# Stick attention begins with the gate projection: a written-out opening of the stage's order

## The reference, cut to what matters

```
def _stick_breaking(q, k, v):                      # 8 heads of 64
    for blk in range(s // SB_BLOCK):               # 8 blocks of 128 queries
        z = einsum('bhqd,bhkd->bhqk', q[:, :, q0:end], k[:, :, :end]) * scale
        log_keep = where(mask, log_sigmoid(-z), 0.0)
        rest = cumsum(log_keep, axis=3, reverse=True) - log_keep
        a = where(mask, exp(log_sigmoid(z) + rest), 0.0)
        outs.append(einsum('bhqk,bhkd->bhqd', a, v[:, :, :end]))
...
q_b = swapaxes(_rms(qkv_b[:, :, 0], sb_q_gain), 1, 2)
k_b = swapaxes(_rms(qkv_b[:, :, 1], sb_k_gain), 1, 2)
o_b = o_b * silu(z_b)
o_a = _rms(o_a, dn_out_gain) * silu(z_a)
gates = sigmoid(proj[..., B_Z1:G1] + b_gate)       # 2048 columns of xn @ w_in
```

## Time and profile before

| | |
|---|---|
| median of 3 runs | 2778.96 us (2775.7 to 2780.8) |
| profiled execution, its own time | 2784.54 us |
| its span, first to last instruction | 2782.6 us |
| PE busy in the span | 2615.7 us (94%) |
| DVE, ACT, POOL busy | 1263.3, 938.4, 352.8 us |
| mean granted TensorE clock | 0.968 |
| stick phase: first instruction, last sigmoid of the gates | 685.56 us, 1056.33 us |

### The profile page before, as it was taken

The page is one execution under the profiler, slowest core; times in us unless marked ns, Lnnn a source line. Parts: engine busy times, 40 slices in busy tenths (PEclk is TensorE's granted clock), DMA queues, the critical chain, the costliest instruction groups (busy, mean ns, idle before and its releaser), DMA issues. The chain is left out here.

```text
span 2782.6 us, 36583 instructions
## 1 busy us (share of the span) xinstructions
PE 2615.7 (94%) x14702; PEld 2245.0 (81%) x14702; DVE 1263.3 (45%) x1770; ACT 938.4 (34%) x1549; POOL 352.8 (13%) x450
## 2 busy tenths in 40 slices
PE   8969999998799998999997989889999999999999
PEld 6849999997588886888886877767888888778877
DVE  6523444442466764543136858454233222323452
ACT  4223322221456652123115767532212111222331
POOL 1002232220332320001012223010000000000000
PEclk9979999999799998999998989989999999999999
DMA  4222121112333215443323211163222222355532
GB/s 144 86 75 82 53 77 49 53 43 64 103 117 92 74 56 185 148 137 101 122 97 102 56 41 39 35 215 92 68 69 76 71 81 68 112 180 171 189 102 80
DMA packets 215503, 264.71 MB, mean 95 GB/s; under 512 B 46852, under 2 KB 147844, under 8 KB 215336
## 3 DMA queue, kind: packets, MB, share of 16 engines
q1 hardware_dynamic: 215336, 262.38, 29.6%
HBM read 185.11 MB, written 77.22 MB: 94 GB/s over the span
## 5 line engine op out<-in xcount | busy, mean ns | idle before, releaser
L3801 PE MATMUL ffn_up_acc<-mixed_hi,ffn_ring_hi 128*128 128x512 f32 x704 | 274.9, 390 | 2.5 <-DVE mixed_lo L2922 2.5
L3801 PE MATMUL ffn_up_acc<-mixed_hi,ffn_ring_lo 128*128 128x512 f32 x704 | 274.6, 390 | 0.0
L3801 PE MATMUL ffn_up_acc<-mixed_lo,ffn_ring_hi 128*128 128x512 f32 x704 | 274.5, 390 | 0.0
L1379 PE MATMUL delta_acc<-delta_w_hi,xn_hi 128*128 128x256 f32 x640 | 192.0, 300 | 2.9 <-DVE delta_w_lo L1333 2.9
L1381 PE MATMUL delta_acc<-delta_w_hi,xn_lo 128*128 128x256 f32 x640 | 181.5, 284 | 0.0
L1380 PE MATMUL delta_acc<-delta_w_lo,xn_hi 128*128 128x256 f32 x640 | 181.4, 283 | 0.0
L3801 PEld LDWEIGHTS ffn_up_acc<-mixed_hi,ffn_ring_hi 128*128 128x128 f32 x704 | 132.6, 188 | 30.2 <-issue 2.9
L3801 PEld LDWEIGHTS ffn_up_acc<-mixed_lo,ffn_ring_hi 128*128 128x128 f32 x704 | 132.6, 188 | 27.5
L3801 PEld LDWEIGHTS ffn_up_acc<-mixed_hi,ffn_ring_lo 128*128 128x128 f32 x704 | 132.5, 188 | 27.5
L4060 DVE TENSOR_TENSOR ffn_feed_lo<-ffn_feed_raw,ffn_feed_hi 128x1536 fp32r<-128x1536 f32 x44 | 77.4, 1759 | 148.1 <-ACT ffn_feed_hi L4052 148.0
L3771 DVE TENSOR_SCALAR ffn_conv<-ffn_padded,ffn_taps 128x1024 f32<-128x1024 f32 x22 | 16.6, 753 | 276.3 <-ACT ffn_padded L3752 276.3
(11 more groups left out here) (444 smaller groups left out, 6449.7 us busy)
## 6 DMA issues: line engine op xcount, KB each, us to landing
ffn_feed_raw<-in_w_down SPq DMA_DIRECT2D x44, 512.0 KB, 3.9
ffn_ring_raw<-in_w_gate SPq DMA_DIRECT2D x11, 1024.0 KB, 5.3
ffn_ring_raw<-in_w_up SPq DMA_DIRECT2D x11, 1024.0 KB, 5.8
scratch_act_t<-ffn_silu SPq DMA_DIRECT2D x22, 512.0 KB, 2.7
ffn_feed_raw<-scratch_act_t SPq DMA_DIRECT2D x44, 256.0 KB, 3.0
delta_w_raw<-in_w_in SPq DMA_DIRECT2D x20, 512.0 KB, 4.0
scratch_projected<-delta_out SPq DMA_DIRECT2D x80, 128.0 KB, 1.7
stick_g_raw<-in_w_in SPq DMA_DIRECT2D x16, 512.0 KB, 4.6
```

Of the source, the lines that this page charges most:

```text
L1379: nc.tensor.matmul(acc, self.hi[:, k, tok], w_hi, start=(k == 0), stop=False, skip_group_check=True)
L3801: last = nc.tensor.matmul(self.acc[s][:, br, cols], weight[:, k, ch], part[:, k, cols], start=(k == 0 and first), stop=(k == 7 and weight ...
```

## The change

Stage 0 gets one more `yield` in its opening on each engine: tile 0's preparation is one part, and tile 1's load, sum, power and scale are the other. On SP the load of tile 1 now stands ahead of the load of v. The plan is written anew: three gate steps, the first part of the opening, two gate steps, then steps with a gate step behind every second of the first 16, and behind each from then on.

```
@@ StickAttention.sync
         self.prep.load(sp, 0)
         self.prep.load_gains(sp)
+        yield
+        self.prep.load(sp, 1)
         sp.dma_start(self.v_sb[:], ...).then_inc(self.v_in, 16)
-        self.prep.load(sp, 1)
@@ gpsimd
-        for j in range(2):
-            self.prep.inverses(pool, j)
+        self.prep.inverses(pool, 0)
+        yield
+        self.prep.inverses(pool, 1)
@@ tensor
             prep.turn(pe, 0, s)
+        yield
         for i in range(self.steps()):
@@
-def even_plan(first, second):
-    plan, given = [], 0
+def stick_plan(first, second):
+    plan = [1, 1, 1, 0, 1, 1]
+    ahead = plan.count(1)
+    late = first - (second - ahead)
     for i in range(first):
         plan += [0, 2]
-        want = second * (i + 1) // first
-        plan += [1] * (want - given)
-        given = want
+        want = min(second, ahead + (i + 1) // 2 if i < 2 * late else ahead + i + 1 - late)
+        plan += [1] * (want - plan.count(1))
     return plan
```

More of the change, by code:

```diff
@@ L4493, in two_blocks @@
                 branch_gates = BranchGates(ph, nc, stick, o_a, z_a, qkv_z_b[:, 1536:], a["dn_out_gain"], gated)
-                run_stages(ph, [stick, gate, branch_gates], even_plan(stick.steps(), gate.steps()))
+                run_stages(ph, [stick, gate, branch_gates], stick_plan(stick.steps(), gate.steps()))
         x1, z2 = scratch("x1", SEQ, D), scratch("z2", SEQ, 1952)
```

## The result

The changed kernel takes 2797.23 us (median of 4 runs, 2790.91 to 2799.58), the kernel before beside it 2779.82 (4 runs, 2775.7 to 2780.8): a ratio of 1.0063, 95% interval 1.0048 to 1.0078. It is slower by 17 us, where 8 were forecast; the time lies 1 us above the range.

What follows compares the result with a forecast made beforehand. PE, busy 94% of the span, was taken as the bound, idle only in the opening's latency chain. Opening 2.2, slots 3.3, steps without turns 1.8, stage 2 1.5, less 0.4, gave +8.4: 2787.4 us, range 2774 to 2796.

Steps and rivals of the forecast that it cites:

- the thinned steps: First 16 steps, a gate group behind every second only: PE left uncovered for ACT's and DVE's latency, in slot and other waits.
- The late opening: Phase start: x waits on SP behind a gate store, five groups move into the hole, the phase ends 2.2 us later.
- The fourth group: Gate group behind tile 0's turns: 2.9 us at full clock, 5.3 at the lower, taken as 4.1.
- The table load: ACT's only table load, ahead of the first gate sigmoid: 0 or 1.28 us exposed, taken whole.
- slots: Tiles 0 and 1, two shared PSUM slots: second turn of a pair waits 1.1 us, three pairs, 3.3 us.
- steps without turns: First 16 steps: without a gate group each pair exposes 0.46 us, four pairs, 1.8 us.
- stage 2: Moved to shorter tiles: ACT waits for the load of `a_z` in step 5, 1.5 us, bounds 0 and 6.
- less 0.4: Taken off the sum for two short waits that the dense plan had in these steps.
- From step 16 both plans have PE full: Later plan, from step 16 on: priced at nothing; a step where cover fails costs 0.46 us.
- Rival "even": Fronts come early and thinned steps cost nothing: 2775.5 us, with half of it 2778 to 2783; chance 0.22.
- Rival "faster": Opening: x held back not at all or much less than 18 us, so PE's idle is filled; 2771 us, chance 0.10.
- Rival "stage 2 binds": Tiles 0 and 1: POOL's chain and loads hold ACT, tile 2's scale holds step 8's turn; +18, 2797 us, chance 0.13.

Runs made afterwards that it cites:

- e5: Kernel before, with four gate groups placed in the opening's own waits and seven picked steps without a gate group; 2762.26 us, ratio 0.9929 to the kernel before.
- e9: Changed kernel, opening kept, its eight steps without a gate group put past tiles 0 and 1, away from hand-overs; 2781.22 us, ratio 1.0010 to the kernel before.
- e7: Changed kernel with stage 2's four POOL products per tile cut to a few columns, all waits kept; 2790.38 us, ratio 1.0035 to the kernel before.
- e1: Changed kernel, opening kept, the 60 gate steps left spread evenly over all 68 steps; 2791.80 us, ratio 1.0044 to the kernel before.
- e8: Kernel before with the first gate weights and bias asked for between the two parts of the opening; 2779.60 us, ratio 0.9997 to the kernel before.
- e2: Changed kernel with each store of gates issued one gate step later on SP; 2785.67 us, ratio 1.0023 to the kernel before.
- e3: Kernel before, opening in the old order, with only the first 16 steps thinned and groups given back right behind; 2789.83 us, ratio 1.0038.

## Why the prediction was wrong

The direction was right, and so were the chain of the opening and its price. The size was 9 us short, and nearly all of that lies in one term, the thinned steps: 6.2 us in the sum, 14.9 measured.

- *The late opening, 2.2 us: right in sum, in its parts with some luck.* x asked for behind the store at 702.1, PE idle for 8.22 and 11.14 us, the turn of step 0 at 737.5. The single steps missed by up to 2.5 us, both ways, and nearly cancelled. The weights took less than 5.0, since the split began at 689.36, 4.5 us after their issue. The fourth group's clock rose part way, as taken. The square of tile 1 came 5.9 us after its load was asked for (723.58 to 729.52) and not 3.4. The likely cause is the load of v, which I priced at nothing and which was issued right behind it; e5's x of tile 0, issued right behind 512 KB of weights, took 5.2 (684.68 to 689.85). No run takes v away, so this isn't shown. e9 has this opening and few waits behind it: 2.4 us in the phase, and from its turn of step 0 to the last sigmoid 321.0 us, for the 321.2 of the sum.
- *The table load, 0 or 1.28: taken whole, right.* It began only when PE had finished the group (699.76, idle before it ended by PE's last product), so none of it was hidden; the sigmoid followed 1.29 us after its start, with no drain behind it. "ACT's only table load" holds for this phase; the program has ten.
- *The thinned steps: the step that failed.* The prediction put 3.3 for slots, 1.8 for steps without turns and 1.5 for stage 2, less 0.4: 6.2. Measured from e9 to after: 14.9, of them 8.0 of waits, 6.5 of lower clock and 0.5 in the opening. The slot waits were as priced: 1.24, 0.93 and 0.97 us in three pairs, 3.1 for 3.3. The other waits weren't: 7.1 of after's 10.2 us from 740 to 800 (1.4 in e9) stand against the 2.9 left of the sum. I had no term for the wait of `apply` at the hand-over of a tile (1.92), nor for POOL stretching DVE (1.1 of the 1.99 and 1.0 of the 1.92 went with it in e7, where another wait of 1.65 opened). The largest missing term is the clock. I charged it only behind the long idle times of the opening, but it fell twice more: two groups took 5.27 and 4.43 us for 2.88, 3.9 together. Another 1.4 or so is that behind the opening it rose 6.6 us after the turn of step 0 (737.5 to 744.1), in e9 3.8 us after it (736.9 to 740.7).
- *The bounds:* the ones I named, twice 5.1 for the steps and 6 for stage 2, add up to 16.2 and hold the 14.9. That is luck in part, for no part of them stood for a lower clock. The range didn't use them: I closed it at 2796, by the chances of the rivals, which left out the upper bound of my own largest unknown. From 2.2 + 16.2 it would have reached 2797.4.
- *"From step 16 both plans have PE full", no cost: right* for this plan (238.60 of 240 us from 800 on), and wrong as a rule. In e1 and e8 single bare steps right ahead of a hand-over or of a turn that waits for a scale opened waits of 1.8 to 2.9 us with a lower clock behind them. The 0.46 us of the earlier trace rows for a bare step was true of step 22 (the profile counts 0.17 of it as idle time), and I read it as the price of any.
- *Rival "even":* of its terms only the weights came true, and in part (4.5 us for 5.0). The table load stood behind the wait, the fourth group took 3.6 us, the group behind step 1 was at the lower clock again (4.6 us), and the waits were exposed.
- *Rival "faster":* its premise, that SP's ask for x decides alone, is wrong. With x asked for at 688 (e2) the first leg won 3.6 us and not 9.8, since ACT's square stands behind the sigmoid in ACT's queue too. The second leg, which I hadn't counted, won 6.6.
- *Rival "stage 2 binds":* its time (2797) came out, its mechanism only in part. POOL's work matters (e7), but through its effect on DVE's short operations, not by holding the scale of tile 2 and the turn of step 8: no wait for a scale is among PE's between 740 and 800. A hit in the number is no proof of the story.
- *Left open:* thinning costs 12.1 us of phase behind the old opening (e3) and 14.9 behind the new one (e9 to after). By the same working as for e9, from the turn of step 0 on, e3's 12.1 over before are 8.5 of waits and 3.6 of busy time, for 8.0 and 6.5. So the 3 us are the clock: it stayed low longer, 6.8 us at the first pair of gaps after (754.4 to 761.2), 3.4 in e3 (737.6 to 741.0). Why, no run tells.

## What to carry to other kernels

Filler work belongs into a chain's waits, not ahead of the chain: follow each moved step through every in-order queue, for a store on SP and a sigmoid on ACT each held loads and squares behind them, and the turn of step 0 came 27 us later with three groups ahead of its first part and two ahead of its second, but 2.2 us later with four placed in its waits. Give up filler only where no wait is open, not in the step right ahead of a hand-over or of a wait for a scale: the place of seven or eight bare steps was worth 5 to 15 us. Price a gap of about 2 us on a full TensorE as a range, its length and up to 3.4 us more of lower clock: behind such gaps that was nothing (e1, 1.78 us before 746.09), 1.5 and 2.4 us (after), and 3.4 us (e1, a mean of 0.83 over 20 us).

## What the runs showed of the hardware

- TensorE's clock fell after short gaps, too: 0.82 and 1.99 us, with 0.43 us of work between them, took it from 1.00 to 0.50, and it stayed there through the 5.27 us of the next group, in which PE had no gap. In e8 one gap of 2.92 us did it (0.52 behind it). It isn't the gap's length alone: behind 1.80 us in e1 (931.74) it fell to 0.50, behind 1.78 us in the same run (746.09) it stayed at 1.00.
- POOL's products and DVE's short operations slow each other when they run side by side. DVE's scan took 1.02 and 1.48 us instead of 0.42, its product 1.38 instead of 0.27, and one POOL product 2.33 instead of 1.29. The Trainium skill, page "GPSIMD Engine Reference", section "1. Specifications", says that GpSimd shares its SBUF interfaces with VectorE and that they contend when a DVE instruction has two inputs in SBUF. The slowed ones have two each, and without POOL's load they were fast again (e7); by that rule, the trace agrees. It doesn't say who pays: the subtraction at 751.69, with two inputs as well, kept its 1.21 us, and there it was POOL's product that took 2.33; in e9 the same subtraction took 1.47 (761.92) and 1.70 us (792.67) beside a POOL product.
